# ScalarE takes the first tap of two depthwise convolutions and the squares of a channel norm; 96 increments ahead of TensorE's program go

## What is computed

```python
def token_mixing(x, ...):
    z = x @ w_in + b_in                       # split into z_a, z_b, z_g, q, z_m
    u = z_a[..., :D_A] * sigmoid(z_a[..., D_A:])
    c_a = causal_depthwise_conv([buf_a, u], w_conv_a, b_conv_a)      # 31 taps, 512 channels
    y_a = silu(layer_norm(c_a, ln_a_g, ln_a_b)) @ w_a_out            # norm over channels
    c_b = causal_depthwise_conv([buf_b, z_b], w_conv_b, b_conv_b)    # 4 taps, 1024 channels
    h   = rg_lru(c_b, h0, w_a, b_a, w_x, b_x, lam)
    y_b = (h * gelu(z_g)) @ w_b_out
    y_c = attention(q, mem_k, mem_v) @ w_c_out                       # 4 heads, 256 memory tokens
    g = sigmoid(z_m)                                                 # three gates per channel
    return (g[0] * y_a + g[1] * y_b + g[2] * y_c) @ w_mix_out
```

## Time and profile before

| what | us |
|---|---|
| median of 3 runs | 1938.06 (1937.14 to 1939.76) |
| profiled execution, its own time | 1935.44 |
| span of that execution | 1933.7 |
| PE busy | 1806.9 (93%) |
| DVE busy | 1454.7 (75%) |
| ACT busy | 1049.9 (54%) |
| mean granted PE clock | 0.976 |

### The profile page before, as it was taken

One profiled execution on the slowest core, in us unless ns is written; L12 is line 12 of the kernel. 1 busy time (PEld: TensorE's weight loads), 2 busy tenths in 40 slices (PEclk: granted clock), 3 DMA queues, 4 the chain that ended last, 5 costly groups with the idle time before them and its releaser, 6 DMA issues. The chain is left out here.

```text
span 1933.7 us, 30371 instructions
## 1 busy us (share of the span) xinstructions
PE 1806.9 (93%) x11505; PEld 1564.9 (81%) x11506; DVE 1454.7 (75%) x2077; ACT 1049.9 (54%) x1188; POOL 135.6 (7%) x159
## 2 busy tenths in 40 slices
PE   6998999899998998999969988999999999999993
PEld 6887899799987988899857777878788888888782
DVE  5999686665535999867576666888888888886766
ACT  4453754444324444474444565777767676775553
POOL 1110000000001011000012002020202020100000
PEclk9999999999999999999979999999999999999997
DMA  6564344354443564544336779999999999996763
GB/s 254 200 227 181 119 148 142 109 173 147 150 143 115 191 218 151 190 141 136 130 113 244 275 247 347 358 355 356 349 360 351 376 330 382 324 384 222 277 239 90
DMA packets 119392, 447.09 MB, mean 231 GB/s; under 512 B 11056, under 2 KB 11184, under 8 KB 118784
## 3 DMA queue, kind: packets, MB, share of 16 engines
q1 hardware_dynamic: 112288, 424.45, 60.3%
q0 software_dynamic: 7008, 21.34, 3.4%
HBM read 435.68 MB, written 12.67 MB: 232 GB/s over the span
## 5 line engine op out<-in xcount | busy, mean ns | idle before, releaser
L646 DVE TENSOR_TENSOR wpl<-e_ring,wph 128x2048 fp32r<-128x2048 f32 x269 | 606.9, 2290 | 93.1 <-ACT wph L640 92.2
L640 ACT CAST wph<-e_ring 128x2048 fp32r<-128x2048 f32 x269 | 502.1, 1904 | 133.4 <-PE psum L2044 68.0
L590 DVE TENSOR_TENSOR wl<-ring,wh 128x1024 fp32r<-128x1024 f32 x234 | 284.9, 1222 | 200.9 <-ACT wh L584 200.3
L1774 PE MATMUL psum<-xTh,wh 128*128 128x320 f32 x1184 | 375.4, 317 | 41.4 <-DVE wl L590 20.6
L1775 PE MATMUL psum<-xTl,wh 128*128 128x320 f32 x1184 | 370.0, 312 | 0.0
L1776 PE MATMUL psum<-xTh,wl 128*128 128x320 f32 x1184 | 369.8, 312 | 0.0
L584 ACT CAST wh<-ring 128x1024 fp32r<-128x1024 f32 x234 | 243.5, 1046 | 160.7 <-PE psum L1795 71.8
L2042 PE MATMUL psum<-wph,xe 128*128 128x512 f32 (+1 forms) x768 | 297.2, 387 | 16.7 <-issue 12.0
L2043 PE MATMUL psum<-wph,xe 128*128 128x512 f32 (+1 forms) x768 | 291.8, 380 | 0.0
L2044 PE MATMUL psum<-wpl,xe 128*128 128x512 f32 (+1 forms) x768 | 290.5, 378 | 0.0
L1774 PEld LDWEIGHTS psum<-xTh,wh 128*128 128x128 f32 x1184 | 226.0, 191 | 54.0 <-DVE wl L590 30.0
(11 more groups left out here) (319 smaller groups left out, 2269.8 us busy)
## 6 DMA issues: line engine op xcount, KB each, us to landing
e_ring<-experts SPq DMA_DIRECT2D x264, 1024.0 KB, 6.3
ring<-stream SPq DMA_DIRECT2D x274, 512.0 KB, 3.3
lnp<-rows POOLq DMA_DIRECT2D x4, 1024.0 KB, 6.3
x<-x POOLq DMA_DIRECT2D x3, 512.0 KB, 5.3
arena<-x0T SPq DMA_DIRECT2D x2, 640.0 KB, 6.0
o_a<-arena POOLq DMA_DIRECT2D x2, 540.0 KB, 6.7
o_k<-arena POOLq DMA_DIRECT2D x2, 512.0 KB, 6.0
o_v<-arena POOLq DMA_DIRECT2D x2, 512.0 KB, 7.3
```

What stands on the lines that cost most here:

```text
L590: dve.tensor_tensor(wl[:, q % SPLITS, :], ring[:, u % SLOTS, :], wh[:, q % SPLITS, :].bitcast(F32), ALU.subtract).then_inc(lo_done, 1)
L640: act.copy(wph[:, SLOT_OF[m % NPOS], :], ring_place(m).rearrange("p u c -> p (u c)")).then_inc(hi_e, 1)
L646: dve.tensor_tensor(wpl[:, s, :], ring_place(m).rearrange("p u c -> p (u c)"), wph[:, s, :].bitcast(F32), ALU.subtract).then_inc(lo_e, 1)
L1774: pe.matmul(out, h[:, k], hi[:, k], start=(k == 0), stop=False)
```

## The change

ACT now writes the first tap of convolution A (`first_tap_a`, tile n-1 behind the sigmoid of tile n, the last one behind the casts for `q`) and of convolution B (`first_tap_b`, tile n-1 behind the eviction of `zb` tile n, the last one behind the wait for the history), each as an Identity with a scale and a bias per partition. It also squares for the channel norm, behind everything in `ATTEND` and ahead of the wait for `var`. DVE loses those instructions and instead waits for ACT at `tap(1)` and at the start of `conv_b`; PE's wait for the squares is now met by ACT. The count of DVE's taps is one lower per layer. The 96 increments ahead of PE's program and their semaphore are gone; those of ACT and DVE stay.

```diff
+                def first_tap_a(j):
+                    act.wait_ge(glu_done, 2 * (JA * l + j + 1))
+                    w, b = col(l, "w_conv_a", K_A * j), col(l, "b_conv_a", j)
+                    act.activation(ca[:, j, 0:SEQ], ua[:, j, 0:SEQ], ACT.Identity, scale=w, bias=b)\
+                       .then_inc(conv_a_first, 1)
+                    act.activation(samp(ca[:, j, SEQ:T]), seg_a(j, 0, DSEQ), ACT.Identity, scale=w, bias=b)\
+                       .then_inc(conv_a_first, 1)
+                def first_tap_b(j):
+                    emptied(act, l, "zb", j)
...
                     frees(act.activation(sg[:, n], bank(l, "za", 2 * n + 1)[:, 0:T], ACT.Sigmoid,
                                          bias=col(l, "b_in", ZA_G + n)), l, "za", 2 * n + 1)
+                    if n:
+                        first_tap_a(n - 1)
                 split_for(tile_of(l, "q", 0).done)
+                first_tap_a(JA - 1)
...
                     frees(ident_bias(seg_b(n, K_B - 1, DSEQ), samp(bank(l, "zb", n)[:, SEQ:T]), b), l, "zb", n)
+                    if n:
+                        first_tap_b(n - 1)
                 act.wait_ge(hist_ready, HIST * (l + 1))
+                first_tap_b(JB - 1)
...
+                emptied(act, l, "mean", 0)
+                act.activation(sg[:], ca[:], ACT.Square).then_inc(dev_ready, 1)
                 made(l, "var", 0)
...
-                    for j in (j0, j0 + 1):
-                        emptied(dve, l, "zb", j)
-                    for k in range(K_B):
+                    dve.wait_ge(conv_b_first, 2 * (JB * l + j0 + 2))
+                    for k in range(1, K_B):
...
-                                if k == 0:
-                                    ins = dve.tensor_scalar(out, in_, w, col(l, "b_conv_b", j), ALU.mult, ALU.add)
-                                else:
-                                    ins = mac(out, in_, w, out)
+                                ins = mac(out, in_, w, out)
...
-                    frees(dve.tensor_scalar(ca[:, j, 0:SEQ], ua[:, j, 0:SEQ], col(l, "w_conv_a", K_A * j),
-                                            col(l, "b_conv_a", j), ALU.mult, ALU.add), l, "za", 2 * j)
-                    ins = dve.tensor_scalar(samp(ca[:, j, SEQ:T]), seg_a(j, 0, DSEQ), col(l, "w_conv_a", K_A * j),
-                                            col(l, "b_conv_a", j), ALU.mult, ALU.add)
-                ins.then_inc(conv_a_tap, 1)
+                    dve.sem_inc(evac[plan.tiles[l, "za", 2 * j].bank], 1)
                 def tap(k):
-                    dve.wait_ge(conv_a_tap, K_A * l + k)
+                    if k > 1:
+                        dve.wait_ge(conv_a_tap, (K_A - 1) * l + k - 1)
                     for j in range(JA):
+                        if k == 1:
+                            dve.wait_ge(conv_a_first, 2 * (JA * l + j + 1))
...
-                        emptied(dve, l, "mean", 0)
-                        dve.tensor_tensor(sg[:], ca[:], ca[:], ALU.mult).then_inc(dev_ready, 1)
...
-            for _ in range(PE_PLACED):
-                pe.sem_inc(pe_placed, 1)
             pe.wait_ge(const_ready, 6)
```

More of the change, by code:

```diff
@@ L113 @@
 SPLIT_AHEAD, LOAD_AHEAD, LATER = 5, 10, 2
-PE_PLACED = 96
 BANK_G, BANK_U, BANK_T, BANK_X, BANK_D, BANK_DB = 0, 1, 2, 3, 4, 6
@@ L511, in trunk @@
         dve_step = sem("dve_step")
-        dve_placed, act_placed, pe_placed = sem("dve_placed"), sem("act_placed"), sem("pe_placed")
+        dve_placed, act_placed = sem("dve_placed"), sem("act_placed")
         spl_exp, spl_ready = sem("spl_exp"), sem("spl_ready")
@@ L518, in trunk @@
         conv_b_done = sem("conv_b_done")
-        conv_a_tap = sem("conv_a_tap")
+        conv_a_tap, conv_a_first, conv_b_first = sem("conv_a_tap"), sem("conv_a_first"), sem("conv_b_first")
         negmax = sem("negmax")
@@ L947, in _ @@
             for l in range(DEPTH):
+                def first_tap_a(j):
[7 more added lines that the diff above has]
+                    emptied(act, l, "zb", j)
+                    w, b = col(l, "w_conv_b", K_B * j), col(l, "b_conv_b", j)
+                    act.activation(cb[:, j, 0:SEQ], zb[:, j, 0:SEQ], ACT.Identity, scale=w, bias=b)\
+                       .then_inc(conv_b_first, 1)
+                    act.activation(samp(cb[:, j, SEQ:T]), seg_b(j, 0, DSEQ), ACT.Identity, scale=w, bias=b)\
+                       .then_inc(conv_b_first, 1)
                 for n in range(JA):
@@ L1044, in _ @@
                                          bias=col(l, "b_rg_a", n)), l, "rg", n)
-                act.wait_ge(conv_a_tap, K_A * (l + 1))
+                act.wait_ge(conv_a_tap, (K_A - 1) * (l + 1))
                 act.wait_ge(tails_ready, 2 * (JA + JB) * (l + 1))
@@ L1359, in _ @@
                                              in1=sg[:, j, 0:SEQ], op0=ALU.add, op1=ALU.mult).then_inc(glu_done, 1)
-                    dve.wait_ge(glu_done, 2 * (JA * l + j) + 1)
                     dve.scalar_tensor_tensor(out=seg_a(j, K_A - 1, DSEQ), in0=samp(z[:, SEQ:T]), scalar=b,
@@ L1423, in _ @@
                         filled(dve, l, "mean", 0)
-                        dve.wait_ge(conv_a_tap, K_A * (l + 1))
+                        dve.wait_ge(conv_a_tap, (K_A - 1) * (l + 1))
                         frees(mac(ca[:], over(bank(l, "mean", 0)[:, 0:T], JA), -1.0 / D_A, ca[:]), l, "mean", 0)
-                        emptied(dve, l, "mean", 0)
-                        dve.tensor_tensor(sg[:], ca[:], ca[:], ALU.mult).then_inc(dev_ready, 1)
                 for n in range(H_C):
@@ L1923, in _ @@
                     elif key[0] == "mean":
-                        pe.wait_ge(conv_a_tap, K_A * (l + 1))
+                        pe.wait_ge(conv_a_tap, (K_A - 1) * (l + 1))
                         take(pe, l, "mean", 0)
```

## The result

The change makes the kernel slower: 1957.1 us (1955.0 to 1963.1, 4 runs) against 1938.9 us (4 runs), a ratio of 1.0098 with a 95% interval of 1.0076 to 1.0120. Forecast were 1938.0 us and a range of 1930 to 1945. The profiled execution took 1956.4 us.

What follows compares the result with a forecast made beforehand. PE, busy 93% of the span, was taken as the bound, so only its waits could win time. Layer 0's +1.3 and layer 1's -1.4 us gave -0.1 us, hence 1938.0 us, range 1930 to 1945.

Steps and rivals of the forecast that it cites:

- The rest: Added waits, PE's increments, expert loop's entry: no effect; PE's program 96 instructions shorter, its 10.2 us entry stall unchanged.
- Rival 3: Expert loop stalls fetching instructions: +5 us if at the entry alone, +12 to +60 in all small turns; 11%.
- Rival 2: Expert loop's entry gets cheaper by up to its 10.2 us stall, giving 1928 to 1934 us; 14%.
- Nothing by themselves: Start of PE's program: the 96 increments ran while PE waited for its first operand, so removing them wins nothing.
- First taps on ScalarE: Convolution B: 0.8 us a pair on ACT delays a cast; PE starts the g stage 0.3 us later in both layers.
- Convolution A: First taps: three of four pairs win nothing; one cast comes later, DVE loses 0.3 us, which its next gaps absorb.
- Rival 4: ACT becomes the new bound, casts queue behind taps: +4 to +6 us in all, 1943 us; 11%.
- rival 1: Tap delays vanish and the clock at 773.7 keeps its level too: -4.4 us, 1933.6 us; 12%.
- First taps off VectorE: Convolution B, waits at 184.50 and 793.61: 0.1 us sooner in layer 0; 0.95 us plus 1.7 us of clock in layer 1.
- The square: On ACT behind branch 2's last gate: variance and square root 1.7 us later; layer 0 +1.3 us, layer 1 without clock +0.3.
- the case that was left open: Branch C: if gate matmuls need the banks of DVE's late evictions, the whole 1.7 us reaches PE.
- The sum: Layer 0 at +1.3 us and layer 1 at -1.4 us give -0.1 us in all.

Runs made afterwards that it cites:

- experiment 4: The kernel before without TensorE's 96 increments and nothing else; 1931.7 us, ratio 0.9970 to the kernel before.
- experiment 1: The changed kernel with 50 more increments in VectorE's idle stretch of layer 0, its loop placed as in the kernel before; 1931.0 us, ratio 0.9962.
- experiment 7: As experiment 1, but convolution A's first taps back on VectorE and 42 increments; 1930.4 us, ratio 0.9959.
- experiment 2: The kernel before with 78 more increments in VectorE's idle stretch, its loop placed as in the changed kernel; 1959.9 us, ratio 1.0105.
- experiment 5: As experiment 1, but the channel norm's square back on VectorE and 48 increments; 1925.2 us, ratio 0.9941.

## Why the prediction was wrong, step by step

**The step that failed: "The rest".** It asked which engine's program the change moves and named PE alone, for its 96 increments. The diff shortens VectorE's program by 50 instructions and lengthens ScalarE's by 52 as well. Rival 3 had the mechanism, turns without instruction packets that must fetch, and a price of 12 to 60 us that holds the 25 measured. But it put it on PE, where nothing happened, gave it 11%, and left the case of all turns out of the range. Instruction packets in the small turns even stood among the signs of being wrong. The moved taps were counted as VectorE's time and never as VectorE's code. Rival 2 does not hold: the entry's wait is 9.87 us, where it was 10.2.

**The increments.** "Nothing by themselves" is wrong. The earlier trace rows show PE only from 164 us on; no row was read at the start. The first row of PE's timeline before is at 15.65 us, and VectorE had the first half of the input done some 8 us earlier, which these two rows would have told. Measured: 3.3 us at the start, 5.6 us in the medians of experiment 4.

**First taps on ScalarE.** The size was right: 0.60 and 0.44 us each, about 0.9 for a pair started back to back, inside the 0.65 to 0.95 taken from the earlier trace rows and above the 0.8 used. Convolution B's two groups in the changed kernel:

```profile
L960 ACT ACTIVATE arena<-arena,par 128x256 f32<-128x256 f32 x8 | 4.8, 601 | 0.0
...
L962 ACT ACTIVATE arena<-arena,par 128x64 f32<-128x64 f32 x8 | 3.5, 437 | 0.0
```

The mechanism holds too. The wait at 120 us grows from 0.88 us (experiment 4) to 1.70 us (experiment 1), and against experiment 4 (160.30) the gate stage starts 0.3 us later in the changed kernel (160.59) and 0.5 us later in experiment 1 (160.83), where +0.3 was said. Convolution A is worth nothing, as said (experiment 7). Rival 4 does not hold: the casts come late, but the gaps take part of it, and behind 791.58 the clock keeps its upper level. Of rival 1, one condition came true in this trace, the upper clock behind the start of layer 1's gate stage; the other, that the tap delays vanish, did not.

**First taps off VectorE.** Forecast were 0.1 us in layer 0 and 0.95 us plus 1.7 us of clock in layer 1. Layer 1's wait became 0.96 us, as forecast (0.95), at the upper clock. Layer 0 was mis-sized: 3.3 us. I had taken the 1.33 us before 184.50 for a property of the code. It was one of the run: in the kernel before, the gates ahead of it ran at the lower clock for 6.9 us, which gave VectorE time to catch up. In experiment 4, the same code with about half of that piece, the wait is 2.36 us, the twin of layer 1's. The eight such waits in the four traces with these taps on VectorE go the same way: 1.33 and 1.35 us behind a long piece, 2.18 to 2.36 us behind one half as long (five waits), and 3.88 us behind none (experiment 2, layer 0).

**The square.** The wait came out as told: ScalarE's square stands right behind the last gate, and PE waits for it. The root was to move by 1.7 us. Before, it started 2.2 us behind the last gate's sigmoid (201.46 and 203.62); now it is 5.9 us, 3.7 more, since the variance ran at the lower clock here (0.66 on the mean from 198 to 203 us). In experiment 1, at the upper clock, it is 2.0 us more.

```profile
196.70 0.53 ACT L1029 ACTIVATE arena<-psum,par 128x320 f32<-128x320 f32 x1 [2.06 <-PE psum L1792]
197.12 1.26 ACT L1048 ACTIVATE arena<-arena 128x1280 f32<-128x1280 f32 x1
198.40 1.28 ACT L1050 ACT_TABLE_LOAD   x1
202.58 0.53 ACT L1050 ACTIVATE arena<-psum,eps_c 128x320 f32<-128x320 f32 x1 [2.90 <-PE psum L1776]
```

PE waits 1.78 us for the variance, 0.37 us for the `wl` behind the root's chain (0.75 said) and 1.02 us for VectorE's evictions, the case that was left open, though that last wait is there in experiment 5 as well, without ScalarE's square. Forecast were +1.3 us a layer against the old place; experiment 5 gives 1.9 us in layer 0 and 4 to 5.9 in all, since a lower clock came with it in layer 1.

**The sum.** The sum of the moves came out as forecast: experiment 1 and experiment 4 differ by all the moves together and stand at 1931.0 and 1931.7 us, where -0.1 was forecast. But that is luck: it is a sum of two terms that were both too small, about -7 us for convolution B and +4 to +6 for the square. The kernel's end was decided by neither.

## What to carry to other kernels

Whether a loop on the chip stays loaded can hang on where it lies in an engine's program, and any edit ahead of it moves it. Here 50 instructions of VectorE's did harm, while PE's loop moved by 96 and ScalarE's by 52 without a packet in the turns. When instructions are added to or taken from an engine's program, look at that engine's instruction packets inside the loop before and after, and not only at the engine that has the increments. Where they appear, some instructions more in an idle stretch of that engine can settle it: the 50 cost nothing that showed, while 96 increments at the front of PE's program were on the path. And a wait that has a piece of lower clock ahead of it is shorter than the code makes it: size it in the twin stage that has none.

## What the runs showed of the hardware

VectorE's loop of 276 instructions went through the small turns without an instruction packet at five of seven places, and with 25 or 26 packets of 8 KB in five turns at the other two; no place gave anything in between. A loop that stays loaded in three lines of 128 and not in four fits all seven. The stalls after the two taken branches were 4.5 and 6.1 us at the turn shown; the DMA engines were busy 0.92 to 0.94 of the time in such turns. The Trainium skill, "Runtime: NRT & Kernel Launch", section "Instruction fetch mechanics", has such a stall after a taken branch; its two lines of 256 instructions agree neither with packets of 8 KB nor with the slow places. By lines of 256, a loop of 276 would reach into a third from 19 places in a row, and the slow ones are 70, 79 and 207.

An increment of a semaphore took 0.09 us of VectorE's program (the 50 of experiment 1) and 0.15 us of PE's, where the 96 run from 0.9 to 15.4 us.

ScalarE's first tap of 256 columns with a scale and a bias per partition, from SBUF, took 0.60 us, against 0.48 us for the eviction of the same width with a bias alone. The Trainium skill, "ScalarE: Activation LUTs", section "What ACT_TABLE_LOAD costs", counts some 0.09 us for each such operand; the 0.12 us here are near it, though the eviction reads PSUM.
